# RWKV recurrence of a four-layer block: values and keys turned two chunks at a time, the score product kept whole, the inverse written through predicates

## The chip, the cores and the metric

The kernel runs on 1 core of one Trainium2 chip. The metric is the device time of one execution in microseconds. Before the change three runs gave 4173.98, 4181.47 and 4182.22 us; the median is 4181.47.

## The reference, cut to what matters

Two blocks run one behind the other, each with two layers, on 512 tokens of width 1024, all in float32. The change touches one stage of the second block only, which runs once in each of its two layers: the time mix of RWKV-7. For each of 16 heads of width 64 it computes

```python
def step(state, inp):                      # state is 64 x 64
    r_t, w_t, k_t, v_t, a_t, b_t = inp
    sa = einsum('bhvk,bhk->bhv', state, a_t)
    state = state * w_t[:, :, None, :] + sa[..., None] * b_t[:, :, None, :] \
            + v_t[..., None] * k_t[:, :, None, :]
    return state, einsum('bhvk,bhk->bhv', state, r_t)
```

The inputs r, w, k, v, a, b come from projections of the normed input, mixed with the token before. Behind the scan stand a group norm over each head, a bonus term and a gate.

## The kernel before, in words

**Tiling.** Features lie on the 128 partitions and the 512 tokens on the free axis, so a tile of 128x512 holds two heads. The stage works through 8 such pairs of heads (`PAIRS`), and the tokens in 8 chunks of 64 (`C`, `NC`). Within a chunk the recurrence is solved in closed form. With A the strictly triangular product of keys `a` and queries `at_` (the score product, `scores(p, 0)` and its transpose `scores(p, 1)`), the inverse of I - A is needed for all 8 chunks of both heads. It is built by doubling: `xx` holds the inverse of the diagonal blocks, `xt` its transpose, and each of five levels (`INV_LEVELS` 2, 4, 8, 16, 32) adds the off-diagonal blocks of one size.

**One level.** `lower(p, i)` multiplies the part `ct` of A that belongs to the level by `xx` (16 small matmuls, by `products`, L1954). ScalarE copies the result from bank 3 to `pp`. `inverse(p, i)` and `inverse_t(p, i)` multiply it by `xt` from the other side. VectorE adds bank 5 to `xx` (`add_x`, L2371) and bank 4 to `xt` (`add_xt`, L2375). `ct` itself is made by VectorE before each level, as `mabt` times a mask of zeros and ones (`next_ct`, L2366). The first `xx` and `xt` are a masked product plus the identity (two instructions each: L2360 and L2382, L2393 and L2396). The two strict score products, the three others and all masks have one instruction each, `keep_masked`, L2360.

**The chain.** Chunks of a pair depend on each other through `state`. Each chunk has three steps, so a pair has 24: `chain(p, i)` on TensorE (L1931 to L1947), and behind each a small VectorE instruction (`rhs` L2263, `uu` L2265, `state` L2268) that the next step waits for. The chain of pair p-1 is woven into the work of pair p: one step stands behind each of the products in TensorE's order, and the `step(...)` calls of VectorE stand at fixed places in its order. Both orders are written by hand and strictly in order. In what follows, steps 0, 3, 6, ... have the larger TensorE part (four groups, A), steps 1, 4, 7, ... the smallest (B), and steps 2, 5, 8, ... the third (C).

**One pair in TensorE's order.** First the dense part: small products for decay `w` and rate `a`, the projections of k and r (24 matmuls each, L228 to L230), a sum of squares (`ssq`), the projection of v, the gate g and a bonus sum. Then the scores: chain 0, `scores` 0, chain 1, `scores` 1, chain 2, `turned` 0, chain 3, `scores` 2 to 4 with chain 4 to 6 behind them. Then five levels, with `turned` 1 and 2 in the first two. `turned` brings v, b and k from features on partitions to tokens on partitions: 8 matmuls of a 128x64 piece each against a 128x128 matrix (L2015, L2017), into two banks, from which ScalarE copies four quarters (`keep_turned`).

**VectorE's order** for a pair is decays, keys (token shift of k), `kt`, `post(p - 2)` (group norm scale, bias and gate of an earlier pair, L2285 to L2288), the norm of the keys (L2341), shift of r, `at_` (L2350), `rt` (L2353), shift of v, step 0, then masks and levels. **ScalarE** carries the activations, the copies out of PSUM, and the negation of each weight piece (L161) that GpSimd's queue needs before it can add the raw weights on top (L132). **SyncE** loads masks at the stage's start (L1895) and two small tiles per pair.

Of the kernel before, what the change touches and what calls it, by code (L numbers as in the profile page):

```python
# [21 lines left out]
P = 128  # L22
# [1785 lines left out]
def rwkv_b(run, io, l, ws, again, nxt, y_all, y_hi, y_lo, gate):  # L1808

    with ExitStack() as ctx:  # L1810
# [9 lines left out]
        xx, ct = z[:, 0, 1:S + 1], z[:, 1, 1:S + 1]  # L1820
# [4 lines left out]
        lm, cen = sc.sb("lm", [P, 10, C]), sc.sb("cen", [P, P])  # L1825
# [17 lines left out]
        x_made, xt_made, c_ready = sc.sem("x_made"), sc.sem("xt_made"), sc.sem("c_ready")  # L1843
# [12 lines left out]
        for p in range(PAIRS):  # L1856
# [7 lines left out]
            for j in range(3):  # L1864
                order += [(f"t{j}", (p, h), h, p_free) for h in range(2)]
# [27 lines left out]
        def _(sp):  # L1893
            sc.enter_and_clear(sp)
            sp.dma_start(lm[:, :, :], io["b_lm"]).then_inc(const_in, 16)  # L1895
            sp.dma_start(bones[:, :], io["b_bones"]).then_inc(const_in, 16)
# [9 lines left out]
        def _(pe):  # L1906
# [12 lines left out]
            def chain(p, i):  # L1919
# [4 lines left out]
                if i % 3 == 0:  # L1924
                    if i == 0 and p:
                        pe.wait_ge(y_kept, p)
                    if i == 0:
                        pe.wait_ge(xt_made, 6 * (p + 1))
                        pe.wait_ge(*read("t2", (p, 1)))
# [27 lines left out]
            def dense(p):  # L1957
                def decays():
# [3 lines left out]
                    if p:  # L1962
                        pe.wait_ge(f_free, 5 * p)
                        pe.wait_ge(x_made, 5 * p)
# [26 lines left out]
            def scores(p, j):  # L1991
                b, f = p % 2, 5 * p + j
                lhs, rhs_ = ((a, at_[b]), (at_[b], a), (kt, at_[b]), (a, rt[b]), (kt, rt[b]))[j]
                if j == 0:
                    pe.wait_ge(at_made, p + 1)
                    pe.wait_ge(*read("w", p))
                elif j == 1:
                    pe.wait_ge(*read("ssq", p))
                else:
                    pe.wait_ge(f_free, f - 1)  # L2000
                if j == 3:
                    pe.wait_ge(rt_made, p + 1)
                products(2 + j % 2, lhs, rhs_, f_made)

            def turned(p, j):
# [81 lines left out]
            pe.wait_ge(f_free, 5 * PAIRS)  # L2087
# [19 lines left out]
        def _(act):  # L2107
# [36 lines left out]
            def decays(p):  # L2144
                act.wait_ge(lr_made, 2 * p + 1)
                if p:
                    act.wait_ge(c_ready, 5 * p)
# [18 lines left out]
            for p in range(PAIRS):  # L2166
# [34 lines left out]
                do(gg[:, p % 2, :], bank("g", p)[:, :], ACT.Copy, signal=read("g", p))  # L2201
                ws.high(st, n + 4)

                def keep_turned(j):
                    dst = (vt, bt, ktt)[j][p % 2]
                    act.wait_ge(tr_made, 3 * p + j + 1)
                    for i in range(4):

                        g, h = i // 2, i % 2
                        src = bank(f"t{j}", (p, g))[0:C, :].rearrange("p (c h k) -> p c h k", c=4, h=2)[:, :, h, :]  # L2210
                        out = dst[h * C:(h + 1) * C, g * 256:(g + 1) * 256].rearrange("p (c k) -> p c k", c=4)
                        do(out, src, ACT.Copy, signal=read(f"t{j}", (p, g)) if h else None)
# [16 lines left out]
            act.wait_ge(c_ready, LEVELS_ * PAIRS)  # L2229
# [21 lines left out]
        def _(dve):  # L2251
# [54 lines left out]
            dve.wait_ge(const_in, 48)  # L2306
            do(dve.scalar_tensor_tensor(out=cen[:, :], in0=bones[:, :], scalar=-1.0 / C, in1=run.eye[:, :],
                                        op0=ALU.mult, op1=ALU.add), (cen_made, 1))
            for p in range(PAIRS):
# [19 lines left out]
                if p:  # L2329
                    decays()  # L2330
                    keys()
# [6 lines left out]
                if p >= 2:  # L2338
                    post(p - 2)
# [13 lines left out]
                do(dve.tensor_tensor(rt[b], r, e0, ALU.mult), (rt_made, p + 1))  # L2353
                shift(f + 2, "v", p, v, col("mu_v", p))

                def keep_masked(j):

                    dst, m = ((mabt, 0), (xx, 2), (mak[b], 0), (mrb[b], 1), (mrk[b], 1))[j]
                    dve.wait_ge(f_made, 5 * p + j + 1)
                    do(dve.tensor_tensor(chunks(dst), chunks(banks[2 + j % 2][:, :]), each_chunk(lm[:, m, :]), ALU.mult),  # L2360
                       (f_free, 5 * p + j + 1))
# [39 lines left out]
                next_ct(1)  # L2401
# [5 lines left out]
                next_ct(2)  # L2407
# [5 lines left out]
                next_ct(3)  # L2413
# [4 lines left out]
                next_ct(4)  # L2418
# [600 lines left out]
def constants_b():  # L3019
# [17 lines left out]
    lm = [s < t, s <= t, level[1].T, level[1]] + [level[n] for n in INV_LEVELS] + [s == t]  # L3037
    lm = np.stack([m.astype(f) for m in lm], 1)
    bones = (row[:, None] // 64 == row[None, :] // 64).astype(f)
# [56 lines left out]
```

## Time and profile before

| | us |
|---|---|
| profiled execution | 4173.47 |
| its span | 4171.7 |
| three runs | 4173.98, 4181.47, 4182.22 |
| TensorE matmul busy | 3868.6 (93%) |
| VectorE busy | 2112.0 (51%) |
| ScalarE busy | 1712.1 (41%) |

The page gives each engine's busy time as a share of the span. TensorE's share counts overlapping matmuls with modelled ends, so 93% is not 93% of its peak. The time mix stage lies between about 1761 and 2290 us (layer 0) and 3072 and 3600 us (layer 1). In the 40 slices of the page VectorE stands at 6 tenths there, where TensorE stands at 8 and 9. In what follows pair 4 of layer 0 stands for the others: its dense part begins at 2001.13, its scores at 2024.74, and the next pair begins at 2059.98.

### The profile page before, as it was taken

Reading aid. Unit: us, or ns where it says so; the run is one execution under the profiler, and the core shown is the slowest. Engines: PE = TensorE matmul, PEld = TensorE weight load, DVE = VectorE, ACT = ScalarE, POOL = GpSimd, SP = SyncE. Lnnn points to the kernel's source line nnn. Section 1 sums busy time; section 2 is a strip of 40 time slices with the busy share of each in tenths; the row PEclk is TensorE's granted clock in tenths of the full one; section 3 lists DMA queues with packets and bytes.
Section 4 is the critical chain, followed back from the end, with each engine's and each line's share of the span. In section 5 each row is a group of like instructions: output and inputs, shape, how many; then the busy total and the mean of one; then the engine's idle time right before and its main releaser. Section 6 shows DMA issues by size and latency. Waiting matters only on the chain.

```text
span 4171.7 us, 70239 instructions
## 1 busy us (share of the span) xinstructions
PE 3868.6 (93%) x29148; PEld 3135.1 (75%) x29148; DVE 2112.0 (51%) x3719; ACT 1712.1 (41%) x2512; POOL 794.6 (19%) x1108
## 2 busy tenths in 40 slices
PE   5898999999899999999999999998999999989997
PEld 4676778777678877877787778876777787778885
DVE  5575662126533227366664376325546666356603
ACT  3264422336443236445443332235644444342223
POOL 1111222221122221210001222221120000222221
PEclk9999999999999999999999999999999999999998
DMA  8855998975489985832223879986572222679995
GB/s 282 236 118 106 272 292 188 199 171 120 95 175 193 191 172 119 177 86 66 53 52 87 182 161 195 193 183 146 115 170 66 52 55 57 142 153 196 193 191 130
DMA packets 189741, 628.75 MB, mean 151 GB/s; under 512 B 22768, under 2 KB 27888, under 8 KB 189040
## 3 DMA queue, kind: packets, MB, share of 16 engines
q0 software_dynamic: 158976, 549.52, 61.0%
q1 hardware_dynamic: 27888, 70.53, 4.9%
q8 instruction: 232, 3.80, 0.4%
q10 hardware_dynamic: 2560, 4.20, 0.3%
q14 instruction: 85, 0.70, 0.1%
HBM read 612.63 MB, written 2.10 MB: 147 GB/s over the span
## 4 chain that ended last, share of the span: by engine, by line
PE 42%; DVE 10%; ACT 6%; DMA 2%; issue 2%; SPq 0%; DVEq 0%; ACTq 0%; POOL 0%
PE bank L228 11%; PE bank L230 10%; PE bank L229 10%; PE bank L1954 4%; ACT L2112 1%; ACT gate L2112 1%; PE bank L1642 1%; PE bank L1624 1%; DVE rw_z L2371 1%; PE bank L1943 1%; ACT w L2112 1%; PE bank L2015 1%; ACT acc L2112 1%; PE bank L1615 1%; DVE x L392 1%
## 5 line engine op out<-in xcount | busy, mean ns | idle before, releaser
L228 PE MATMUL bank<-h_hi,w_hi 128*128 128x512 f32 x2608 | 1065.7, 409 | 46.4 <-DMA w_lo<-in_b_wup 7.9
L230 PE MATMUL bank<-h_hi,w_lo 128*128 128x512 f32 x2608 | 1024.6, 393 | 0.0
L229 PE MATMUL bank<-h_lo,w_hi 128*128 128x512 f32 x2608 | 1024.4, 393 | 0.0
L161 ACT ACTIVATE w_lo<-w_hi 128x1024 fp32r<-128x1024 f32 (+2 forms) x552 | 556.0, 1011 | 1002.5 <-DMA w_hi<-in_a_wgv 301.8
L228 PEld LDWEIGHTS bank<-h_hi,w_hi 128*128 128x128 f32 x2608 | 494.5, 190 | 180.5 <-issue 57.2
L229 PEld LDWEIGHTS bank<-h_lo,w_hi 128*128 128x128 f32 x2608 | 495.1, 190 | 106.5 <-issue 10.5
L230 PEld LDWEIGHTS bank<-h_hi,w_lo 128*128 128x128 f32 x2608 | 494.4, 190 | 106.9
L2112 ACT ACTIVATE gate<-bank 128x512 f32<-128x512 f32 x80 | 47.8, 597 | 277.1 <-PE bank L1954 277.1
L228 PE MATMUL bank<-fa_y_hi,w_hi 128*128 128x512 f32 x352 | 137.1, 390 | 1.8 <-DMA w_lo<-in_a_wd 1.8
L228 PE MATMUL bank<-fb_y_hi,w_hi 128*128 128x512 f32 x352 | 137.0, 389 | 0.7 <-DMA w_lo<-in_b_wd 0.7
L229 PE MATMUL bank<-fb_y_lo,w_hi 128*128 128x512 f32 x352 | 136.9, 389 | 0.0
L230 PE MATMUL bank<-fb_y_hi,w_lo 128*128 128x512 f32 x352 | 136.9, 389 | 0.0
L230 PE MATMUL bank<-fa_y_hi,w_lo 128*128 128x512 f32 x352 | 136.9, 389 | 0.0
L229 PE MATMUL bank<-fa_y_lo,w_hi 128*128 128x512 f32 x352 | 136.9, 389 | 0.0
L1388 DVE TENSOR_SCALAR fa_conv<-fa_a_in,par_a 128x512 f32<-128x512 f32 x44 | 21.6, 492 | 225.9 <-ACT fa_a_in L1334 225.5
L2637 DVE SCALAR_TENSOR_TENSOR fb_work<-fb_work,par_b 128x512 f32<-128x512 f32 x176 | 132.3, 752 | 6.3
L128 POOL DMA_DIRECT2D w_hi<-in_b_wrkv x48 | 31.5, 655 | 520.6 <-PE bank L230 520.6
L2634 DVE TENSOR_TENSOR fb_work<-bank,rstd 128x512 f32<-128x512 f32 x88 | 60.9, 692 | 124.5 <-PE bank L230 123.7
L2647 DVE COPY fb_work<-bank 128x512 f32<-128x512 f32 x16 | 11.1, 692 | 211.3 <-ACT w L319 211.3
L1421 DVE SCALAR_TENSOR_TENSOR x<-bank,mods,x 128x512 f32<-128x512 f32 x16 | 12.0, 751 | 207.1 <-PE bank L230 207.1
L132 POOL DMA_DIRECT2D w_lo<-in_a_wgv x96 | 90.3, 947 | 125.4 <-ACT w_lo L161 117.9
L132 POOL DMA_DIRECT2D w_lo<-in_b_wup x96 | 87.1, 914 | 115.3 <-ACT w_lo L161 108.1
(461 smaller groups left out, 7661.7 us busy)
## 6 DMA issues: line engine op xcount, KB each, us to landing
w_hi<-in_a_wgv POOLq DMA_DIRECT2D x80, 512.0 KB, 5.3
w_lo<-in_a_wgv POOLq DMA_DIRECT2D x80, 512.0 KB, 7.6
w_hi<-in_b_wup POOLq DMA_DIRECT2D x80, 512.0 KB, 5.2
w_lo<-in_b_wup POOLq DMA_DIRECT2D x80, 512.0 KB, 7.4
w_hi<-in_a_wh POOLq DMA_DIRECT2D x48, 512.0 KB, 4.7
w_lo<-in_a_wh POOLq DMA_DIRECT2D x48, 512.0 KB, 5.7
fa_ada_raw<-in_ada SPq DMA_DIRECT2D x48, 512.0 KB, 7.9
w_hi<-in_b_wrkv POOLq DMA_DIRECT2D x48, 512.0 KB, 4.9
```

What stands on the lines that cost most here:

```text
L132: pool.dma_start(self.lo[:, self.span(n)], self.pieces[n][0], accum_op=ALU.add)\
L161: st.do(st.eng.activation(self.lo[:, s], self.hi[:, s].bitcast(F32), ACT.Copy, scale=-1.0), (self.neg_made, n + 1))
L228: pe.matmul(out, self.hi[:, a], hh[:, k0 + k, :], start=first and k == 0, stop=False)
L229: pe.matmul(out, self.hi[:, a], hl[:, k0 + k, :], start=False, stop=False)
L230: mm = pe.matmul(out, self.lo[:, a], hh[:, k0 + k, :], start=False, stop=last and k == ks - 1)
L392: st.do(st.eng.scalar_tensor_tensor(out=run.x[:, k, :], in0=y, scalar=gain[:, k:k + 1], in1=run.x[:, k, :], op0=ALU.mult, op1=ALU.add), se ...
L1615: mm = pe.matmul(banks[2 + g][:, 256 * j:256 * (j + 1)], rot[rows, p % 2, ib * P:(ib + 1) * P], kpad[rows, kb, ib * P:(ib + 2) * P], start ...
L1624: mm = pe.transpose(banks[4 + i // 4][:, (i % 4) * P:(i % 4 + 1) * P], s[:, u % 3, i * P:(i + 1) * P], run.eye[:, :])
L1954: mm = pe.matmul(banks[out][s_, cut(c)], lhs[s_, cut(c)], rhs_[s_, cut(c)], start=True, stop=True)
L2112: st.do(act.activation(*args, **how), signal)
L2634: do(dve.tensor_tensor(a_in[:, b, 2:S + 2], banks[n % 4][:, :], run.rstd[:, :], ALU.mult), (a_free, n + 1))
L2637: do(dve.scalar_tensor_tensor(out=conv[:, b, :], in0=a_in[:, b, j:j + S], scalar=col(f"conv{j}", n), in1=conv[:, b, :], op0=ALU.mult, op1= ...
```

## The change

Four things, all in the time mix stage. (1) `turned` takes two chunks at once: 4 matmuls with 128 weight columns where there were 8 with 64, into one bank; the four copies of ScalarE keep their size. (2) ScalarE copies the first score product whole from bank 2 to `mabt`, with no mask, and `lower` multiplies all of it. (3) `xx` and `xt` are first filled with identities by ScalarE, and every later write to them is one `copy_predicated` under an integer mask, which takes only the blocks of that level; `ct`, its five masks and the two additions of the identity are gone. (4) In VectorE's order `post(p - 2)` moves from behind `kt` to ahead of the keys, and step 0 of the chain moves ahead of the shift of v. A new constant `im` (128 x 11 x 64, int32) is loaded at the stage's start, and `lm` shrinks from 10 masks to 3.

```diff
@@ rwkv_b: tiles and order
-        xx, ct = z[:, 0, 1:S + 1], z[:, 1, 1:S + 1]
+        xx = [z[:, i, 1:S + 1] for i in range(2)]
-        lm, cen = sc.sb("lm", [P, 10, C]), sc.sb("cen", [P, P])
+        lm, im, cen = sc.sb("lm", [P, 3, C]), sc.sb("im", [P, 11, C], I32), sc.sb("cen", [P, P])
...
-                order += [(f"t{j}", (p, h), h, p_free) for h in range(2)]
+                order.append((f"t{j}", p, j % 2, p_free))
...
@@ sync
             sp.dma_start(lm[:, :, :], io["b_lm"]).then_inc(const_in, 16)
+            sp.dma_start(im[:, :, :], io["b_im"]).then_inc(const_in, 16)
@@ tensor: scores(p, j), turned(p, j), lower(p, i)
                 elif j == 1:
                     pe.wait_ge(*read("ssq", p))
+                elif j == 2:
+                    pe.wait_ge(ab_made, p + 1)
+                elif j == 3:
+                    pe.wait_ge(x_made, LEVELS_ * p + 1)
+                    pe.wait_ge(rt_made, p + 1)
                 else:
-                    pe.wait_ge(f_free, f - 1)
-                if j == 3:
-                    pe.wait_ge(rt_made, p + 1)
+                    pe.wait_ge(f_free, 3 * p + 1)
...
-                outs = [claim(f"t{j}", (p, h)) for h in range(2)]
-                for c in range(NC):
-                    out = outs[c // 4][0:C, (c % 4) * P:(c % 4 + 1) * P]
+                whole_bank = claim(f"t{j}", p)
+                for i in range(NC // 2):
+                    out, two = whole_bank[:, i * P:(i + 1) * P], slice(i * P, (i + 1) * P)
                     if j == 0:
-                        mm = pe.matmul(out, v[:, cut(c)], cen[:, :], start=True, stop=True)
+                        mm = pe.matmul(out, v[:, two], cen[:, :], start=True, stop=True)
                     else:
-                        mm = pe.transpose(out, (e0, e1)[j - 1][:, cut(c)], run.eye[:, :])
+                        mm = pe.transpose(out, (e0, e1)[j - 1][:, two], run.eye[:, :])
...
                 pe.wait_ge(x_made, n + 1)
-                pe.wait_ge(c_ready, n + 1)
...
-                    pe.wait_ge(f_free, 5 * p + 4)
-                products(3, ct, xx, cx_made)
+                    pe.wait_ge(f_free, 3 * p + 2)
+                products(3, mabt, xx[p % 2], cx_made)
@@ scalar: for each pair, behind the copy of g
                 do(gg[:, p % 2, :], bank("g", p)[:, :], ACT.Copy, signal=read("g", p))
+                if p >= 2:
+                    act.wait_ge(ch_made, 24 * (p - 1))
+                else:
+                    act.wait_ge(const_in, 64)
+                do(chunks(xt[p % 2]), each_chunk(lm[:, 2, :]), ACT.Copy, signal=(one_made, 2 * p + 1))
+                act.wait_ge(z_free, f + 2)
+                do(chunks(xx[p % 2]), each_chunk(lm[:, 2, :]), ACT.Copy, signal=(one_made, 2 * p + 2))
+                act.wait_ge(f_made, 5 * p + 1)
+                do(mabt, banks[2][:, :], ACT.Copy, signal=(ab_made, p + 1))
                 ws.high(st, n + 4)
...
@@ vector: for each pair
                 if p:
                     decays()
+                    if p >= 2:
+                        post(p - 2)
                     keys()
...
                 do(dve.tensor_tensor(kt, kp, e1, ALU.mult))
-                if p >= 2:
-                    post(p - 2)
...
                 do(dve.tensor_tensor(rt[b], r, e0, ALU.mult), (rt_made, p + 1))
+                step(0)
                 shift(f + 2, "v", p, v, col("mu_v", p))
...
-                    dst, m = ((mabt, 0), (xx, 2), (mak[b], 0), (mrb[b], 1), (mrk[b], 1))[j]
+                    dst, m = ((mak[b], 0), (mrb[b], 1), (mrk[b], 1))[j - 2]
...
-                def next_ct(i):
-                    if i:
-                        dve.wait_ge(cx_made, LEVELS_ * p + i)
-                    do(dve.tensor_tensor(chunks(ct), chunks(mabt), each_chunk(lm[:, 4 + i, :]), ALU.mult),
-                       (c_ready, LEVELS_ * p + i + 1))
+                def put(dst, m, src, signal):
+                    do(dve.copy_predicated(chunks(dst), each_chunk(im[:, m, :]), chunks(src)), signal)
+
+                def first_x():
+                    dve.wait_ge(f_made, 5 * p + 2)
+                    dve.wait_ge(one_made, 2 * p + 2)
+                    put(xx[b], 0, banks[3][:, :], (x_made, LEVELS_ * p + 1))
+
+                def first_xt():
+                    dve.wait_ge(ab_made, p + 1)
+                    put(xt[b], 5, mabt, (xt_made, 6 * p + 1))
                 def add_x(i):
                     dve.wait_ge(xcx_made, 4 * p + i + 1)
-                    do(dve.tensor_tensor(xx, xx, banks[5][:, :], ALU.add), (x_made, LEVELS_ * p + i + 2))
+                    put(xx[b], 1 + i, banks[5][:, :], (x_made, LEVELS_ * p + i + 2))
                 def add_xt(i):
                     dve.wait_ge(xcxt_made, LEVELS_ * p + i + 1)
-                    do(dve.tensor_tensor(xt[b], xt[b], banks[4][:, :], ALU.add), (xt_made, 6 * p + i + 2))
+                    put(xt[b], 6 + i, banks[4][:, :], (xt_made, 6 * p + i + 2))
-                one = each_chunk(lm[:, 9, :])
-                step(0)
-                keep_masked(0)
                 step(1)
-                keep_masked(1)
-                do(dve.tensor_tensor(chunks(xx), chunks(xx), one, ALU.add), (x_made, LEVELS_ * p + 1))
+                first_x()
                 step(2)
-                next_ct(0)
+                first_xt()
...
-                do(dve.tensor_tensor(chunks(xt[b]), chunks(mabt), each_chunk(lm[:, 3, :]), ALU.mult))
...
-                do(dve.tensor_tensor(chunks(xt[b]), chunks(xt[b]), one, ALU.add), (xt_made, 6 * p + 1))
...
-                next_ct(1)
...
-                next_ct(2)
...
-                next_ct(3)
...
-                next_ct(4)
@@ constants_b
-    lm = [s < t, s <= t, level[1].T, level[1]] + [level[n] for n in INV_LEVELS] + [s == t]
+    lm = [s < t, s <= t, s == t]
+    im = [level[n].T for n in (1,) + INV_LEVELS[:-1]] + [level[n] for n in (1,) + INV_LEVELS]
```

## Rows read from the trace of the kernel before

**Rows 1.** Busy time by stretch: pair 4's dense part, its scores and levels, pair 1, layer 1
```profile
2001.13:2024.74 23.61, 22.25 (x90) 15.55 (x86) 13.68 (x20) 18.72 (x25) 2.83 (x5) 1.00 0.27 68
2024.74:2059.98 35.24, 32.59 (x889) 30.13 (x888) 24.71 (x52) 8.71 (x19) 1.45 (x3) 1.00 0.25 54
...
1849.70:1884.80 35.10, 32.46 (x891) 30.10 (x890) 23.10 (x50) 8.29 (x18) 0.88 (x1) 1.00 0.23 51
...
3072.00:3600.00 528.00, 497.12 (x8016) 407.21 (x8015) 317.55 (x586) 237.50 (x369) 46.98 (x66) 1.00 0.32 73
```

**Rows 2.** The chain of waits through pair 4 of layer 0: start, length, what
```profile
2009.41 0.64 ACT acc L2112
...
2016.27 0.76 DVE y_all L2285
2018.57 0.70 DVE w L2341
...
2025.76 0.70 DVE gate L2277
...
2053.59 0.61 ACT gate L2112
```

**Rows 3.** Groups by form of VectorE: count, busy and mean, idle before
```profile
L2366 DVE TENSOR_TENSOR rw_z<-gate,rw_lm 128x512 f32<-128x512 f32 x80 | 55.4, 693 | 5.6 <-PE bank L1954 2.7 <-DVE rw_rhs L2263 0.2 <-DVE rw_state L2268 0.2
...
L1163 DVE COPY_PREDICATED ma_kept<-ma_masks,bank 128x512 f32<-128x512 int32 x56 | 41.6, 743 | 9.1 <-PE bank L951 3.2 <-DVE ma_decay L1181 0.5
```

**Rows 4.** Timeline of pair 4, VectorE and ScalarE ahead of the scores
```profile
2013.30 0.69 DVE L2277 TENSOR_TENSOR gate<-rw_z 128x512 f32<-128x512 f32 x1 [6.26 <-ACT rw_z L2112]
...
2017.22 0.61 ACT L2112 ACTIVATE rw_z<-bank 128x512 f32<-128x512 f32 x1
...
2024.40 0.60 ACT L2112 ACTIVATE rw_gg<-bank 128x512 f32<-128x512 f32 x1
```

**Rows 5.** Timeline of pair 4, weight loads of TensorE, scores to level 2
```profile
2024.74 0.20 PEld L1931 LDWEIGHTS bank<-rw_state,rw_at 64*64 64x64 f32 x4 [0.76 <-issue]
2025.20 1.06 PEld L1954 LDWEIGHTS bank<-rw_at,gate 64*64 64x64 f32 x32
...
2027.55 0.19 PEld L1939 LDWEIGHTS bank<-rw_rhs,rw_xt 64*64 64x64 f32 x4 [1.28 <-DVE rw_rhs L2263]
2028.59 0.20 PEld L1943 LDWEIGHTS bank<-rw_mrb,rw_uu 64*64 64x64 f32 x4
...
2029.14 1.72 PEld L2015 LDWEIGHTS bank<-rw_cen,gate 128*64 128x64 f32 x16
...
2031.03 0.20 PEld L1931 LDWEIGHTS bank<-rw_state,rw_at 64*64 64x64 f32 x4 [0.17 <-issue]
...
2043.74 0.80 PEld L2017 LDWEIGHTS bank<-eye,w 128*64 128x64 f32 x8
...
2047.85 1.06 PEld L1954 LDWEIGHTS bank<-rw_z 64*64 64x64 f32 x32
```

**Rows 6.** Timeline of pair 4, one level of the inverse (level 3)
```profile
2052.35 1.06 PEld L1954 LDWEIGHTS bank<-rw_z 64*64 64x64 f32 x32
...
2053.28 0.25 PEld L1931 LDWEIGHTS bank<-rw_state,rw_at 64*64 64x64 f32 x4
...
2054.24 1.01 PEld L1954 LDWEIGHTS bank<-gate,rw_xt 64*64 64x64 f32 x32 [0.36 <-ACT gate L2112]
...
2055.17 0.20 PEld L1939 LDWEIGHTS bank<-rw_rhs,rw_xt 64*64 64x64 f32 x4
...
2055.28 1.02 PEld L1954 LDWEIGHTS bank<-rw_xt,gate 64*64 64x64 f32 x32
...
2055.51 0.69 DVE L2371 TENSOR_TENSOR rw_z<-rw_z,bank 128x512 f32<-128x512 f32 x1 [0.66 <-PE bank L1954]
...
2056.51 0.20 PEld L1943 LDWEIGHTS bank<-rw_mrb,rw_uu 64*64 64x64 f32 x4 [0.21 <-DVE rw_uu L2265]
```

**Rows 7.** Timeline, a run of full-width f32 matmuls in an earlier stage
```profile
352.37 1.05 PE L951 MATMUL bank<-ma_sw 128*128 128x128 f32 x8
```

More of the change, by code:

```diff
@@ L1842, in rwkv_b @@
         f_made, f_free, tr_made = sc.sem("f_made"), sc.sem("f_free"), sc.sem("tr_made")
-        x_made, xt_made, c_ready = sc.sem("x_made"), sc.sem("xt_made"), sc.sem("c_ready")
+        x_made, xt_made = sc.sem("x_made"), sc.sem("xt_made")
+        ab_made, one_made = sc.sem("ab_made"), sc.sem("one_made")
         cx_made, cx_kept, xcx_made, xcxt_made = (sc.sem("cx_made"), sc.sem("cx_kept"), sc.sem("xcx_made"),
@@ L1928, in chain @@
                         pe.wait_ge(xt_made, 6 * (p + 1))
-                        pe.wait_ge(*read("t2", (p, 1)))
+                        pe.wait_ge(*read("t2", p))
                     for s_ in heads:
@@ L1962, in decays @@
                     if p:
-                        pe.wait_ge(f_free, 5 * p)
+                        pe.wait_ge(f_free, 3 * p)
                         pe.wait_ge(x_made, 5 * p)
@@ L1991, in scores @@
             def scores(p, j):
-                b, f = p % 2, 5 * p + j
+                b = p % 2
                 lhs, rhs_ = ((a, at_[b]), (at_[b], a), (kt, at_[b]), (a, rt[b]), (kt, rt[b]))[j]
@@ L2086, in last_var @@
                     whole("var", PAIRS - 1, bones[:, :], yq[:, :], var_made)
-            pe.wait_ge(f_free, 5 * PAIRS)
+            pe.wait_ge(f_free, 3 * PAIRS)
             pe.wait_ge(x_made, 5 * PAIRS)
@@ L2146, in decays @@
                 if p:
-                    act.wait_ge(c_ready, 5 * p)
+                    act.wait_ge(cx_made, 5 * p)
                 st.settle()
@@ L2207, in keep_turned @@
                     for i in range(4):
[L2209 to L2212, printed above, removed]
+                        q, h = i // 2, i % 2
+                        src = bank(f"t{j}", p)[q * C:(q + 1) * C, :].rearrange("p (c h k) -> p c h k", c=4, h=2)
+                        out = dst[h * C:(h + 1) * C, :].rearrange("p (c two k) -> p c two k", c=4, two=2)
+                        do(out[:, :, q, :], src[:, :, h, :], ACT.Copy, signal=read(f"t{j}", p) if i == 3 else None)
                 keep_turned(0)
@@ L2228, in _ @@
             keep_y(PAIRS - 2)
-            act.wait_ge(c_ready, LEVELS_ * PAIRS)
+            act.wait_ge(cx_made, LEVELS_ * PAIRS)
             act.wait_ge(xcxt_made, LEVELS_ * PAIRS)
@@ L2305, in _ @@
             shift(2, "low", 2, gd[:, 1, :], col("mu_g", 1))
-            dve.wait_ge(const_in, 48)
+            dve.wait_ge(const_in, 64)
             do(dve.scalar_tensor_tensor(out=cen[:, :], in0=bones[:, :], scalar=-1.0 / C, in1=run.eye[:, :],
@@ L2353, in _ @@
                 do(dve.tensor_tensor(rt[b], r, e0, ALU.mult), (rt_made, p + 1))
+                step(0)
                 shift(f + 2, "v", p, v, col("mu_v", p))
                 def keep_masked(j):
-                    dst, m = ((mabt, 0), (xx, 2), (mak[b], 0), (mrb[b], 1), (mrk[b], 1))[j]
+                    dst, m = ((mak[b], 0), (mrb[b], 1), (mrk[b], 1))[j - 2]
                     dve.wait_ge(f_made, 5 * p + j + 1)
                     do(dve.tensor_tensor(chunks(dst), chunks(banks[2 + j % 2][:, :]), each_chunk(lm[:, m, :]), ALU.mult),
-                       (f_free, 5 * p + j + 1))
@@ L2363, in next_ct @@
-                def next_ct(i):
-                    if i:
-                        dve.wait_ge(cx_made, LEVELS_ * p + i)
-                    do(dve.tensor_tensor(chunks(ct), chunks(mabt), each_chunk(lm[:, 4 + i, :]), ALU.mult),
-                       (c_ready, LEVELS_ * p + i + 1))
+                       (f_free, 3 * p + j - 1))
+                def put(dst, m, src, signal):
[4 more added lines that the diff above has]
+                    put(xx[b], 0, banks[3][:, :], (x_made, LEVELS_ * p + 1))
@@ L3036, in constants_b @@
         level[n] = same & (s % (2 * n) < n) & (t % (2 * n) >= n)
-    lm = [s < t, s <= t, level[1].T, level[1]] + [level[n] for n in INV_LEVELS] + [s == t]
+    lm = [s < t, s <= t, s == t]
     lm = np.stack([m.astype(f) for m in lm], 1)
+    im = [level[n].T for n in (1,) + INV_LEVELS[:-1]] + [level[n] for n in (1,) + INV_LEVELS]
+    im = np.stack([m.astype(np.int32) for m in im], 1)
     bones = (row[:, None] // 64 == row[None, :] // 64).astype(f)
@@ L3041, in constants_b @@
     reset[:, ::C] = 0.0
-    return {"b_freq": freq, "b_band": band, "b_lm": np.concatenate([lm, lm]), "b_bones": bones, "b_reset": reset}
+    return {"b_freq": freq, "b_band": band, "b_lm": np.concatenate([lm, lm]), "b_im": np.concatenate([im, im]), "b_bones": bones, "b_reset": reset}
 def arrays_b(inp):
```

## The prediction

> **What bounds the kernel now.** I read the windows first, then the chain of waits inside one pair, then the timeline. Only the time mix stage is touched, about 528 us in each of two layers [rows 1]. Pair 4 splits into a dense part of 23.61 us and 35.24 us of scores, levels and chain steps; pair 1 takes 35.10 for the latter [rows 1]. In neither part is one engine simply full. In the second, matmuls are recorded busy for 32.59 of 35.24 us, but a small matmul's record outlasts its slot in the queue: a group of 16 (a "product") starts at 2052.35 and the next instruction at 2053.28, so it costs 0.93 of TensorE's order, although its weight loads alone are recorded at 1.06 [rows 6]. The chain of waits passes back and forth: ScalarE's variance work and VectorE's `post` and norm, a shift of v, then in the levels ScalarE's copy [rows 2]. So the reader is to see a loop between three in-order queues, where an edit is worth what the last wait at each place loses.
>
> **Prices.** From starts of weight loads: product 0.93; step A 0.46 (2024.74 to 2025.20) [rows 5]; step B 0.11 (2055.17 to 2055.28) [rows 6]; step C I take at 0.34 from the same pace. From a product's start to a reader: 1.27 on VectorE (2054.24 to 2055.51), 1.24 on ScalarE (2052.35 to 2053.59) [rows 2, 6]. A masked product on VectorE costs 0.693, a predicated copy of 128x512 from PSUM under an int32 mask 0.743: the same form runs 56 times in an earlier stage [rows 3]. ScalarE's copy of a bank costs 0.61 [rows 2].
>
> **Part 1, turned in pairs.** `turned` 0 holds the order from 2029.14 to 2031.03, 1.89 for 16 records; a transposing one records 0.80 for its 8 loads, some 0.95 of the order [rows 5]. Half the matmuls of the same moving width is half of that, if twice the weight columns cost nothing. A run of 8 full-width f32 records took 1.05 including the last one's latency [rows 7], which is a pace no worse than 0.12. So 0.95, 0.5 and 0.5: it saves 1.9 a pair. Bounds: nothing saved (weights twice as long in the way) and 1.9. I take the latter, since the full-width row is the same instruction. The Trainium skill ("TensorE: Matmul & The Clock Gate", section "LDWEIGHTS (loading the stationary operand)") says that a weight load takes time in proportion to its columns, whatever the contraction. By that rule eight loads of 64 columns and four of 128 cost the same, and wherever loads set the pace this part would save nothing; the full-width row, at the pace of the half-width one, speaks for loads that are hidden.
>
> **Part 2, the front of the pair.** Today `post` (2.3 us, 2016.27 to 2018.57) stands between `kt` and the norm [rows 2]. Its input is ready at 2010.05 (ScalarE's exponential from 2009.41) [rows 2], and VectorE idles 6.26 us until 2013.30 [rows 4]. Moved there, `post` ends near 2012.4 and is hidden with 0.9 to spare; were that cover gone, it would cost what it overruns. What is late next is the copy of r, from 2017.22 to 2017.83 [rows 4]: the shift of r can start at 2017.9 where it started 2.3 - 0.9 = 1.4 later. The whole train behind it moves up by about 1.5, so `at_` ends near 2023.5 and `rt` near 2024.2, before TensorE leaves the dense part, which stays at 2024.74. Today `at_`, `rt` and the shift of v run until 2027.25, and only then comes step 0 (the wait of 1.28 ahead of 2027.55) [rows 2, 5]. After: step 0 at 2025.33 to 2025.55, shift of v to 2027.05, step 1 to 2027.30. TensorE: A 2024.74, `scores` 0 2025.20, B 2026.13, `scores` 1 2026.25, then C waits for step 1 until 2027.36. It began at 2028.59 [rows 5]: 1.23 gained. `turned` 0 then ends at 2028.65 where it ended at 2031.03 [rows 5], 1.15 more (0.95 of it part 1, the rest a gap of 0.2 ahead of it).
>
> **Part 3, scores 2 to level 2.** VectorE loses ten instructions (two masked first products, the masked first `xt`, two identity additions, five `ct`), gains two predicated writes, and nine additions become predicated: so 19 instructions of 0.693 become 11 of 0.743, 13.2 becomes 8.2 us [rows 3]. ScalarE gains three copies, 1.9 us. Walked in order with the prices above: step 3 at 2028.65, `scores` 2 at 2029.11, B 2030.05, `scores` 3 2030.16, then C waits 0.45 for step 4 (which stands behind the third mask, ready at 2031.24) until 2031.55; `scores` 4 2031.89, A 2032.83, level 0 2033.29, B 2034.23, `turned` 1 2034.34, C 2035.13 (0.29 waited), inverse 2035.47, A 2036.41, its transpose 2036.87, B 2037.81, level 1 2037.92, C 2039.19 (0.33), `turned` 2 2039.53, A 2040.25, and so on to level 2 at 2043.37. From the end of `turned` 0 that is 14.7 us; before, from 2031.03 to 2047.85, 16.82 [rows 5]. Gained: 2.1, of it 0.95 part 1.
>
> **Part 4, levels 2 to 4.** Nothing is gained. A level takes 4.50 (2047.85 to 2052.35) [rows 5, 6]; its waits are ScalarE's copy (0.36 ahead of 2054.24) and `uu` behind `add_x` (0.21 ahead of 2056.51) [rows 6]. `ct` lay in VectorE's idle time. Both waits stay, and `add_x` as a predicated copy is 0.05 longer: 0.15 lost a pair, three levels.
>
> **Moves that I cost at nothing.** ScalarE's three copies stand behind the copy of g (2024.40) [rows 4]. The two identities are read first at 2027.5 and 2028.6 and made by 2026.0; `mabt` is made at 2027.05 and `scores` 2 comes at 2029.11. Slack 1.5 to 2 us; if it were gone, each microsecond would hold `scores` 2 and all behind it by one, some 15 us in all. Behind ScalarE's new waits (previous chain, shift of r, `scores` 0) stand one negation L161 and GpSimd's L132, both 2 us later, for weights used 30 us on. `scores` 2 now waits for `mabt`, with chain 4 behind it; `scores` 3 for `xx`, ready at 2028.3. The mask load adds one DMA of 360 KB to SyncE's queue ahead of the others, while the weight queue has a third of the DMA time [rows 1]; the first use of a predicate comes over 40 us later in layer 0.
>
> **Sum.** Walk per pair 24.74 to 55.65 against 24.74 to 59.98: 1.23 + 1.15 + 2.1 - 0.15 = 4.3 us. But the same walk made over the kernel before gives 34.3, 0.9 short of 35.24 [rows 1]; the rest are short gaps, ahead of `turned` above all, which the change will not remove. I charge 0.6 of it: 3.75 a pair. Six pairs (2 to 7) give 22.5; pair 1, without `post`, 3.5 (35.10 against 30.9 + 0.6) [rows 1]; pair 0 has no chain, so only part 1 less the longer adds, 1.5. That is 27.5 a layer, 55 in both. The profiled execution took 4173.5, 8 us under the median of 4181.5 and level with the fastest of the three runs: 4118.5 by the one, 4126.5 by the other. I give the middle, 4122.
>
> **Rivals.**
> *Half of it (4148).* The full-width weight load isn't hidden: part 1 saves nothing, 1.9 a pair over 16 pairs, 30 us less. The row for full width [rows 7] speaks against; for it, that row's operands are other tiles and its run is short. The same size would follow if ScalarE's slack at `scores` 2 were overrun by 2 us.
> *More of it (4105).* The gaps go too, because fewer claims and waits stand ahead of `turned`: 4.3 to 4.7 a pair, 15 us more.
> *Nothing (4178).* The loop is set by the chain of `state` alone, so that each step waits for the one before. Against: in rows 6 TensorE waits 0.36 and 0.21 in 4.5, the rest is its own work.
> *Slower (4212).* The predicated copy is dearer here than the 0.743 of its twin, since the mask repeats every 64 elements and the target is read and written in place. Its price stands in the wait of every `uu` and `rhs`. Walking with 1.0 gives 32.5 a pair, with 1.2 34.0, and at 1.25 the gain of VectorE is spent (34.3 for the old kernel by the same walk). At twice 0.743, 1.5, the walk is 36.5, 2.2 longer a pair, 30 us in all. Against it speaks only that row, but it differs in nothing else.
>
> **Chances.** Forecast 0.62, half 0.17, more 0.12, nothing 0.04, slower 0.05. About 0.2% (8 us) is what a measurement can tell from no change. Faster by more 0.91, within 0.04, slower 0.05. The range takes in "more" with 5 us for which level of the runs is met, and "half": 4096 to 4150.
>
> **What would show it.** `turned` 0 in half its time; C(2) within 2.7 us of A(0) where it was 3.85; predicated copies at 0.74 to 0.75; levels 2 to 4 at 4.5 to 4.6 as before; the second part of a pair at 31.5; dense part unchanged at 23.6; stage near 500 us. I am wrong if the dense part grows (`post` in the way of the keys), if ScalarE ends the wait of `scores` 2, or if the stages behind give back what the recurrence gained, since their weights must still be loaded.

## The result, and the profile after

The changed kernel takes 4121.16 us (median of 4 runs, 4118.63 to 4127.93), the kernel before 4177.73 beside it (4 runs, 4172.39 to 4182.22): the recorded ratio is 0.9876, with a 95% interval of 0.9862 to 0.9889 (the quotient of the two medians is 0.9865). The profiled execution took 4121.49 us where that of before took 4173.5, 52 us less.

The stretches of the changed kernel, in the columns of [rows 1]: pair 4's dense part, pair 4's scores and levels, those of pair 5. The granted clock of TensorE is 1.00 in each, as in [rows 1], so it has no part in the difference.

```profile
1986.59:2010.27 23.68, 22.27 (x91) 15.56 (x87) 14.67 (x21) 19.05 (x26) 3.39 (x5) 1.00 0.30 71
2010.27:2042.61 32.34, 30.36 (x873) 28.34 (x872) 18.67 (x42) 10.26 (x21) 0.87 (x1) 1.00 0.24 56
2065.95:2097.27 31.32, 30.21 (x873) 28.26 (x873) 18.69 (x42) 10.26 (x21) 0.87 (x1) 1.00 0.25 57
```

The dense part is where it was (23.61 to 23.68) and all the gain lies behind it: 35.24 to 32.34 in pair 4, and 31.32 in pair 5; pair 4 holds one gap of 1.02 us that pair 5 lacks. Over the twelve pairs 1 to 6 of both layers the median of the second part is 31.46, and 34.93 before. Pair 0 falls from 46.8 and 47.38 (its two layers) to 44.72 and 44.75. From the start of pair 0 to the start of pair 7 the stage is 22.9 and 22.2 us shorter (394.77 and 394.2 to 371.86 and 372.01); on to the last step A, pair 7 and its chain bring 3.8 and 3.5 more. That makes 52.4 us, and the 52.0 of the span follow from it only because the rest nearly cancels: between the two stages the changed kernel takes 6.5 us longer (816.9 for 810.3), ahead of the first 1.8 us less and behind the second 4.3 us less (575.9 for 580.3). Over the thirteen kernels of this document, which are built alike there, these stretches lie between 810 and 818 and between 574 and 580 us, in one profiled execution each. So the gain of the stages is not visibly given back, but no run excludes that a few us of it are.

The weight loads of TensorE in pair 4 answer to [rows 5]: from step A of chunk 0 to the next step A, and then the start of level 2 and of level 3.

```profile
2010.27 0.20 PEld L1933 LDWEIGHTS bank<-rw_state,rw_at 64*64 64x64 f32 x4 [0.76 <-issue]
2010.73 1.06 PEld L1956 LDWEIGHTS bank<-rw_at,gate 64*64 64x64 f32 x32
2011.66 0.25 PEld L1941 LDWEIGHTS bank<-rw_rhs,rw_xt 64*64 64x64 f32 x4
2012.90 0.19 PEld L1945 LDWEIGHTS bank<-rw_mrb,rw_uu 64*64 64x64 f32 x4
2013.44 0.97 PEld L2020 LDWEIGHTS bank<-rw_cen,gate 128*128 128x128 f32 x8
2014.53 0.20 PEld L1933 LDWEIGHTS bank<-rw_state,rw_at 64*64 64x64 f32 x4
...
2021.40 0.42 PEld L2022 LDWEIGHTS bank<-eye,w 128*128 128x128 f32 x4
...
2030.38 1.06 PEld L1956 LDWEIGHTS bank<-rw_z,gate 64*64 64x64 f32 x32
...
2034.59 0.19 PEld L1945 LDWEIGHTS bank<-rw_mrb,rw_uu 64*64 64x64 f32 x4 [0.26 <-DVE rw_uu L2278]
...
2034.93 1.06 PEld L1956 LDWEIGHTS bank<-rw_z,gate 64*64 64x64 f32 x32
```

Step B has no wait any more, where 1.28 stood ahead of it, and so step C follows 2.63 after step A (3.85 before). `scores` 2 (the product behind the step A of 2014.53) has no wait for ScalarE's copy either. `turned` 0 holds the order for 1.09 (2013.44 to 2014.53; 1.89 before), a transposing one records 0.42 for 4 loads (0.80 for 8). Level 2 takes 4.55 (2030.38 to 2034.93; 4.50 before) and waits 0.26 for `uu` (0.21 before).

VectorE's timeline of the pair shows `post` (the tail of a group norm, its first instruction L2298) in what was idle time, step 0 at 2010.85, and the first predicated copy:

```profile
1995.30 0.75 DVE L2298 SCALAR_TENSOR_TENSOR y_all<-y_all,par_b,acc 128x512 f32<-128x512 f32 x1 [3.09 <-ACT acc L2116]
...
2010.85 0.23 DVE L2276 COPY rw_rhs<-bank 128x64 f32<-128x64 f32 x1 [1.00 <-PE bank L1934]
...
2013.07 0.74 DVE L2378 COPY_PREDICATED rw_z<-rw_im,bank 128x512 f32<-128x512 int32 x1 [0.23 <-PE bank L1956]
2013.85 0.28 DVE L2281 SCALAR_TENSOR_TENSOR rw_state<-rw_state,rw_ec,bank 128x64 f32<-128x64 f32 x1
```

The groups of predicated copies (count, busy, mean in ns, idle before them), from a bank and from `mabt` in SBUF, and ScalarE's copies of the ones:

```profile
L2378 DVE COPY_PREDICATED rw_z<-rw_im,bank 128x512 f32<-128x512 int32 x80 | 59.0, 737 | 82.8 <-PE bank L1956 82.8
L2378 DVE COPY_PREDICATED rw_xt<-rw_im,bank 128x512 f32<-128x512 int32 x80 | 58.9, 736 | 24.1 <-PE bank L1956 21.8
L2378 DVE COPY_PREDICATED rw_xt<-rw_im,gate 128x512 f32<-128x512 int32 x16 | 11.8, 736 | 0.6
L2116 ACT ACTIVATE rw_z<-rw_lm 128x512 f32<-128x512 f32 x16 | 10.1, 632 | 1.5
```

What TensorE waits for in the time mix stage of layer 0 (total us, times, longest), first in the kernel before:

```profile
PE bank L1939 <- DVE rw_rhs L2263: 7.9, 13, 1.2
...
PE bank L1943 <- DVE rw_uu L2265: 2.6, 7, 0.4
...
PE bank L1931 <- DVE rw_state L2268: 2.0, 8, 0.5
```

and after. The wait for `rhs`, 1.2 us once in each of pairs 2 to 7, is the one that went. The listed waits for VectorE fall by 11 us in eight pairs and the stage by 26.7: the rest is TensorE's own work and waits too short for this view.

```profile
PE bank L1956 <- ACT gate L2116: 5.2, 17, 0.7
...
PE bank L1941 <- DVE rw_rhs L2276: 1.1, 7, 0.2
PE bank L1933 <- DVE rw_state L2281: 0.5, 1, 0.5
```

### The profile page after: what moved, and what is told of

It is laid out like the page before. It is cut to its first block, busy times and chain, and to the rows that moved or that the text cites. A ratio compares the mean times of both kernels' runs of the same rounds, so it can differ in the third digit from the quotient of the medians.

```text
span 4119.7 us, 69619 instructions
## 1 busy us (share of the span) xinstructions
PE 3838.9 (93%) x28892; PEld 3113.2 (76%) x28892; DVE 2031.1 (49%) x3591; ACT 1740.7 (42%) x2560; POOL 792.4 (19%) x1108
## 4 chain that ended last, share of the span: by engine, by line
PE 48%; ACT 5%; DVE 5%; DMA 2%; issue 1%; SPq 0%; ACTq 0%; DVEq 0%; POOL 0%
PE bank L228 11%; PE bank L230 11%; PE bank L229 11%; PE bank L1956 5%; ACT gate L2116 1%; PE bank L1642 1%; PE bank L1919 1%; PE bank L1945 1%; ACT L2116 1%; PE bank L1624 1%; DVE rw_z L2378 1%; PE bank L1615 1%; DMA at_sw<-at_raw 1%; ACT acc L2116 1%; PE bank L1933 0%
## 5 line engine op out<-in xcount | busy, mean ns | idle before, releaser
L2116 ACT ACTIVATE gate<-bank 128x512 f32<-128x512 f32 x96 | 57.3, 597 | 267.0 <-PE bank L1956 266.8
L319 ACT ACTIVATE w<-x 128x512 f32<-128x512 f32 x72 | 45.5, 632 | 151.0 <-DVE x L1421 72.0
```

Source lines behind the costliest of these rows:

```text
L319: st.do(st.eng.activation(self.run.w[:, k % 2, :], src, ACT.Square), self.sig("sq", 8 * part + k + 1))
L2116: st.do(act.activation(*args, **how), signal)
```

## The experiments

For each kernel I read off the weight loads the time from one step A (line 1931 or 1933) to the next: eight segments a pair. Medians over the twelve pairs 1 to 6; the first segment holds `scores` 0 and 1 and `turned` 0, the second `scores` 2 to 4, the third the start of level 0 and `turned` 1, the fourth the rest of level 0, the start of level 1 and `turned` 2, then the later levels. "sum" adds the eight medians, so it leaves out gaps that stand in a few pairs only.

```
kernel        A0-A3 -A6  -A9  -A12 -A15 -A18 -A21 -end  sum   time us  ratio to before, 95%
before        6.29  4.09 4.99 4.31 4.05 4.50 4.50 2.20  34.93 4177.73
after         4.26  4.06 3.64 3.96 4.10 4.55 4.55 2.20  31.32 4121.16  0.9876 0.9862-0.9889
only_turned   5.96  4.18 4.97 3.90 4.05 4.50 4.50 2.20  34.26 4160.62  0.9982 0.9972-0.9991
only_order    5.79  4.05 5.01 4.31 4.05 4.50 4.50 2.20  34.41 4165.46  0.9987 0.9975-0.9998
only_masks    6.28  4.05 3.99 4.36 4.10 4.55 4.55 2.20  34.08 4160.21  0.9972 0.9962-0.9981
no_turned     5.07  4.05 3.99 4.36 4.10 4.55 4.54 2.20  32.86 4147.53  0.9945 0.9928-0.9961
no_order      5.46  4.06 3.65 3.96 4.10 4.55 4.55 2.20  32.53 4143.01  0.9925 0.9899-0.9951
no_masks      5.13  4.18 4.97 3.90 4.05 4.50 4.50 2.20  33.43 4154.31  0.9952 0.9935-0.9968
twice         4.68  5.01 3.64 5.11 5.44 5.44 5.44 2.17  36.93 4209.45  1.0080 1.0054-1.0107
uu_first      4.26  4.06 3.64 3.61 4.03 4.27 4.28 2.17  30.32 4109.43  0.9843 0.9818-0.9868
both_orders   4.26  3.93 3.58 3.61 4.02 4.12 4.15 2.20  29.87 4109.44  0.9863 0.9845-0.9881
no_post       4.67  4.18 3.65 3.96 4.10 4.55 4.55 2.20  31.86 4138.97  0.9928 0.9908-0.9948
no_step0      4.08  4.07 3.64 3.96 4.10 4.55 4.55 2.20  31.15 4121.64  0.9887 0.9867-0.9907
```

The kernel before ran again beside each set of experiments (medians 4173.12, 4171.68 and 4167.65; 4177.73 beside the changed kernel), and the ratio is to those runs. So a difference in us between two rows can be off by up to 10 us where the rows come from different sets; there the ratios and the segments decide.

**One part alone.** My theory was the loop between queues; the rivals were that TensorE's work or VectorE's work alone sets the time.

only_turned, the kernel before with pairs of chunks turned:

```diff
-                for c in range(NC):
-                    out = outs[c // 4][0:C, (c % 4) * P:(c % 4 + 1) * P]
+                for i in range(NC // 2):
+                    out, two = whole_bank[:, i * P:(i + 1) * P], slice(i * P, (i + 1) * P)
```

> The kernel before with part 1 alone (chunks turned in pairs). Loop theory (a step is worth what the last wait at its place loses): TensorE gets 1.9 us a pair back, but VectorE is the late one until level 2, so the second part of a pair falls only from 34.9 to 34.3, pair 0 keeps its 1.5 to 2, and the whole is 10 to 14 us faster than before. TensorE theory (93% busy, its work decides): the full 1.9 x 16 = 30 us.

Second part 34.29, so 0.64 a pair of the 1.9 of TensorE's order that the part takes out. The medians lie 12.5 us apart, inside what the loop theory gave; the ratio says 7.5 us (4 to 12). Both exclude the 30 us of the TensorE theory. The weight loads of pair 4 in it show where the rest goes:

```profile
2022.34 0.19 PEld L1939 LDWEIGHTS bank<-rw_rhs,rw_xt 64*64 64x64 f32 x4 [1.29 <-DVE rw_rhs L2263]
...
2023.93 0.97 PEld L2015 LDWEIGHTS bank<-rw_cen,gate 128*128 128x128 f32 x8
2025.51 0.20 PEld L1931 LDWEIGHTS bank<-rw_state,rw_at 64*64 64x64 f32 x4 [0.61 <-DVE rw_state L2268]
```

`turned` 0 is short, and the next step A then waits 0.61 for `state`: VectorE hands on late.

only_order, the kernel before with `post` ahead of `keys` and step 0 ahead of the shift of v:

```diff
+                    if p >= 2:
+                        post(p - 2)
                     keys()
...
+                step(0)
                 shift(f + 2, "v", p, v, col("mu_v", p))
```

> The kernel before with the two moves in VectorE's order alone (post ahead of the keys, chain step 0 ahead of the shift of v). Loop theory: the first wait goes (1.2 us), but the two masked products and the identity behind it take most of it back, second part 34.9 to 34.4, 5 to 8 us in all. Rival, the front's gain is kept whole: 1.2 x 14 = 17 us.

34.41, as the walk had it; the first segment falls by 0.5, and the medians lie 7.7 us apart (5 us by the ratio), where the rival had 17.

only_masks, the kernel before with `mabt` and the ones by ScalarE and predicated copies:

```diff
-                    do(dve.tensor_tensor(xx, xx, banks[5][:, :], ALU.add), (x_made, LEVELS_ * p + i + 2))
+                    put(xx[b], 1 + i, banks[5][:, :], (x_made, LEVELS_ * p + i + 2))
```

> The kernel before with the masks' part alone (whole score product kept by ScalarE, identities by ScalarE, predicated copies). Loop theory: VectorE has 5 us less a pair, but it starts late into the scores (step 0 stands behind post and the shift) and TensorE has the long turned; second part 34.9 to 34.1, 9 to 13 us in all. VectorE theory (its work in this stage decides): 5 us x 16 x most of it, 50 us or more, nearly all of what the change brought.

34.08. Five microseconds less of VectorE's work a pair are worth 0.85 and 13 us in all, where the rival that counts VectorE's work had 50 or more: it falls. The gain lies in one segment (4.99 to 3.99). The first doesn't move, since the 1.27 ahead of step B is still there.

**One part taken back from the changed kernel.** If the parts simply added, taking one out would cost what it brought alone.

no_turned (the `-` and `+` lines of only_turned exchanged):

> The changed kernel with the old turned (8 matmuls of 64 columns). Loop theory: VectorE is early now, so TensorE's 1.9 us count nearly whole: second part 31.4 to 33.2, 25 to 30 us slower than the changed kernel (4147 to 4152). If the three parts simply add up, it loses what part 1 alone brings, 10 to 14 us.

no_order (those of only_order exchanged):

> The changed kernel with VectorE's old order (post behind kt, step 0 behind the shift of v). Loop theory: second part 31.4 to 32.7, 14 to 18 us slower than the changed kernel (4135 to 4139). If the parts add up: it loses only what the moves alone bring, 5 to 8 us.

no_masks (the old masks, `ct` and additions, the rest of the change kept):

```diff
-                    put(xx[b], 1 + i, banks[5][:, :], (x_made, LEVELS_ * p + i + 2))
+                    do(dve.tensor_tensor(xx, xx, banks[5][:, :], ALU.add), (x_made, LEVELS_ * p + i + 2))
```

> The changed kernel with the old masks, ct and additions (parts 1 and the order kept). Loop theory: second part 31.4 to 33.6, 30 to 35 us slower than the changed kernel (4151 to 4156). VectorE theory: nearly all of the 56 us is gone. If the parts add up: 9 to 13 us slower.

Taken out, the parts cost 1.5, 1.2 and 2.1 a pair (no_turned, no_order, no_masks against after), near what the loop theory had for each (1.8, 1.3 and 2.2); alone they bring 0.67, 0.52 and 0.85. So they don't add: alone 2.0 together, the whole change 3.6. By the medians the three are 26, 22 and 33 us slower than the changed kernel; no_order was expected at 14 to 18, and 22 (20 by the ratio) lies above that. The rival in no_masks, that nearly all of the gain is VectorE's work and goes with it, falls: 33 of some 57 us went. The ratios say the same of the sum: 0.18, 0.13 and 0.28% alone, 0.69, 0.49 and 0.76% taken out, 1.24% in all. The first segment shows it best: 6.29 falls by 0.33, 0.50 and 0.01 with one part, and by 2.03 with all three. It ends with the later of two things, TensorE's own order (with its wait for `rhs`) and `state` from VectorE, and each part shortens only one. In no_masks the waits show the shift: ahead of step B 1.1 in all is left, but ahead of step C, which needs `uu` from a VectorE busy with masks, there is now 10.6 (2.6 before):

```profile
PE bank L1943 <- DVE rw_uu L2265: 10.6, 20, 0.8
...
PE bank L1939 <- DVE rw_rhs L2263: 1.1, 7, 0.2
```

**The two moves apart.** no_post puts `post` back behind `kt` and leaves step 0 where the change has it:

```diff
-                    if p >= 2:
-                        post(p - 2)
...
                 do(dve.tensor_tensor(kt, kp, e1, ALU.mult))
+                if p >= 2:
+                    post(p - 2)
```

> The changed kernel with post back behind kt, step 0 still ahead of the shift of v. The walk: at_ late again by 1.4, but step 0 at once behind rt, so step C(2) waits 0.4 more; second part 31.4 to 31.8, 6 us slower than the changed kernel. Rival (the prediction's text put the 1.23 down to both moves together): most of the 1.3 is lost, second part 32.7.

no_step0 puts only step 0 back behind the shift of v:

```diff
-                step(0)
                 shift(f + 2, "v", p, v, col("mu_v", p))
...
+                step(0)
                 step(1)
```

> The changed kernel with step 0 back behind the shift of v, post still moved. The walk: with at_ early, the shift of v ends near 2025.8 on pair 4's clock and step 0 still comes before TensorE has finished the first score product; no loss, second part 31.3 to 31.4, within 2 us of the changed kernel. Rival: step 0's place is what brought the gain, second part 32.7.

With step 0 behind the shift nothing is lost in time (4121.64 us), and the first segment is even 0.18 shorter (4.08 for 4.26): in the changed kernel VectorE stands idle for 1.00 until TensorE's step A is through (the row of 2010.85). Only then comes the shift of v, and `uu` behind it is a little late for step C, which follows 2.63 after step A in the changed kernel and 2.45 in no_step0. With `post` back 0.54 of segment time a pair and 18 us in all (22 by the ratio) are lost, at least three times what I expected in time. The two profiled executions place most of it: the span is 16.8 us longer, 13.6 of it in the two stages. Pairs 1 to 6 hold 9.2 (6.5 by the segments, the rest is gaps put down to "issue", of which no_post has eight over 0.25 us and the changed kernel three), pair 7 3.3 and pair 0 1.4. Both moves back cost 1.2 a pair, though: once `post` is late, step 0's place matters. Pair 1, which has no `post` ahead of it, is the cross-check: in no_order its first segment takes 4.08 where the other pairs take 5.46, in no_post 4.27 where they take 4.67. no_post's timeline of pair 4 shows `rt` (L2366) running until 2016.22 with step 0 on its heels; the step would have had to stand behind the whole shift of v:

```profile
2015.27 0.20 PEld L1933 LDWEIGHTS bank<-rw_state,rw_at 64*64 64x64 f32 x4 [0.76 <-issue]
...
2015.53 0.69 DVE L2366 TENSOR_TENSOR rw_rt<-gate,w 128x512 f32<-128x512 f32 x1
...
2016.26 0.22 DVE L2276 COPY rw_rhs<-bank 128x64 f32<-128x64 f32 x1
...
2018.30 0.19 PEld L1945 LDWEIGHTS bank<-rw_mrb,rw_uu 64*64 64x64 f32 x4 [0.46 <-DVE rw_uu L2278]
```

**The price of the predicated copy.** twice makes each of them two times:

```diff
-                    do(dve.copy_predicated(chunks(dst), each_chunk(im[:, m, :]), chunks(src)), signal)
+                    for sig in (None, signal):
+                        do(dve.copy_predicated(chunks(dst), each_chunk(im[:, m, :]), chunks(src)), sig)
```

> The changed kernel with each predicated copy made twice (the second writes the same again), 1.5 us in place of 0.74, the price at which I said that the change turns slower. Loop theory: second part 31.4 to 37.0, 80 to 90 us slower than the changed kernel, 25 to 35 slower than the kernel before. Rival: VectorE has idle time in the levels that takes up the second copy (5 us of idle a pair), under 30 us slower than the changed kernel.

88 us slower than the changed kernel (85 by the ratio), 0.8% slower than before; 36.93 a pair, and the wait of step C for `uu` now leads:

```profile
PE bank L1945 <- DVE rw_uu L2278: 27.4, 35, 1.2
PE bank L1933 <- DVE rw_state L2281: 9.4, 29, 0.5
```

This was the prediction's slower case with its price of 1.5 made true, and the walk held: 36.5 plus the 0.6 charged, and 4212 us. The point at which the gain is spent, put at a price of 1.25, was not run.

**A better order.** In a level `uu` stood on VectorE behind `add_x`. uu_first puts steps 10, 13, 16 and 19 ahead of the copy that they stood behind:

```diff
                 step(9)
+                step(10)
                 add_xt(0)
-                step(10, 11)
+                step(11)
                 step(12)
-                add_x(1)
                 step(13)
+                add_x(1)
                 add_xt(1)
                 step(14, 15)
-                add_x(2)
                 step(16)
+                add_x(2)
                 add_xt(2)
                 step(17, 18)
-                add_x(3)
                 step(19)
+                add_x(3)
                 add_xt(3)
```

> The changed kernel with the chain's copy (uu) ahead of the predicated write of xx or xt in levels 1 to 3 and once in level 0. Loop theory: the wait of 0.24 to 0.26 ahead of step C goes, and the next product still finds xx ready or misses it by under 0.1: 0.2 to 0.3 us in four places, second part 31.4 to 30.5, 10 to 14 us faster than the changed kernel. Rival: the product waits for xx by as much as the chain gained, no change.

30.32 a pair, 1.0 less than the changed kernel, and 4109.43 us. On VectorE in level 2 `uu` comes first, and step C follows 1.05 after step B (2032.24), where it took 1.39 in the changed kernel (2033.20 to 2034.59); from step A to step A it is 4.26 (4.55):

```profile
2030.56 0.20 PEld L1933 LDWEIGHTS bank<-rw_state,rw_at 64*64 64x64 f32 x4
...
2032.24 0.20 PEld L1941 LDWEIGHTS bank<-rw_rhs,rw_xt 64*64 64x64 f32 x4
...
2032.70 0.22 DVE L2278 COPY rw_uu<-bank 128x64 f32<-128x64 f32 x1 [1.33 <-PE bank L1941]
2032.95 0.73 DVE L2378 COPY_PREDICATED rw_z<-rw_im,bank 128x512 f32<-128x512 int32 x1
2033.29 0.20 PEld L1945 LDWEIGHTS bank<-rw_mrb,rw_uu 64*64 64x64 f32 x4
...
2034.82 0.20 PEld L1933 LDWEIGHTS bank<-rw_state,rw_at 64*64 64x64 f32 x4
```

both_orders also takes step 4 ahead of the third mask, and in levels 2 and 3 lets TensorE take two chain steps before the product that waits for ScalarE (VectorE's steps 17 and 20 move ahead of a copy to match):

```diff
+                    if i in (2, 3):
+                        chain_on()
+                        inverse(p, i)
+                        chain_on()
+                        inverse_t(p, i)
+                        continue
...
-                keep_masked(2)
                 step(4)
+                keep_masked(2)
```

> uu_first, and in addition chain step 4 ahead of the third mask on VectorE, and in levels 2 and 3 on TensorE a second chain step ahead of the product that waits for ScalarE's copy. Loop theory: the wait of 0.3 ahead of C(5) goes, and step B fits into the wait for the copy, so second part 30.4 to 29.4 (levels 2 and 3 from 4.3 to 4.1 each), 12 to 17 us faster than uu_first, 4093 to 4100. Rival: the levels are bound by product, copy, product, write of xx, so that only step 4's 0.3 shows (5 us).

29.87, half of the 1.0 that I expected over uu_first: levels 2 and 3 give 0.15 and 0.13, step 4 gives 0.13, since the score behind it then waits for the mask. The 12 to 17 us expected in time did not come: 4109.44 against 4109.43. Gaps took back what the segments gained; with them the median of the second part is 30.36 here and 30.39 in uu_first. So uu_first is the version to keep. Its ratio lies below the changed kernel's, but the intervals overlap a little (up to 0.9868 against 0.9862 upwards), and the two come from different sets; the 12 us rest on the 1.0 a pair of the segments and on the two stages, which are 12.5 us shorter in its profiled execution.

## Why the prediction was right

The forecast was 4122, the time is 4121.16. That they agree within 1 us is luck: executions of the changed kernel alone spread over 9 us, and the forecast was the middle of two levels 8 us apart. What was right is the size, 52 to 57 us, and the walk behind it. By its steps:

- *Prices.* The predicated copy 0.737 for 0.743, ScalarE's copy of the ones 0.632 for 0.61. Right.
- *Part 1.* `turned` 0 holds the order 1.09 where I had 0.95, and the 0.2 between step C and it stayed (2012.90 to 2013.44 is 0.54, as 2028.59 to 2029.14 in [rows 5]). Here the first segment is 4.26 and the walk had 3.91. The doubled weights cost next to nothing: in `turned` 0 the records of 64 columns start 0.109 apart, those of 128 columns 0.111. So the first reason of "half of it" is excluded; the second, ScalarE late for `scores` 2, is too, since no wait of TensorE for ScalarE stands ahead of it in any pair. By the section "LDWEIGHTS (loading the stationary operand)" of the page "TensorE: Matmul & The Clock Gate" in the Trainium skill, eight loads of 64 columns would take as long as four of 128. The records here don't halve the spacing with the columns (0.42 for four of 128 against 0.80 for eight of 64), and one record lasts 0.192 for 128 columns and 0.137 for 64. So twice the columns did not slow TensorE's queue here; what sets the spacing, and whether the load inside a record follows the rule, no run here shows.
- *Part 2.* Right in size: step C 2.63 after step A, 2.62 forecast. Wrong in part of its cause: the text credits the moves of `post` and of step 0 together, and beside the first the second brings nothing and costs 0.18 of the first segment (no_step0); it would matter only without the first (no_order against no_post, 0.67 a pair). The train behind `post` moved up by so much that `rt` and the shift of v are out of the way by themselves.
- *Part 3.* From the end of `turned` 0 to level 2: 2014.53 to 2030.38 is 15.85, 14.83 without the gap of 1.02; the walk had 14.7. The gain is smaller than the 2.1 forecast all the same, 1.7: the 16.82 of the kernel before holds a gap of its own in pair 4 (0.30, put down to "issue", ahead of 2034.29), which the median pair lacks.
- *Part 4.* A level went from 4.50 to 4.55, the 0.05 forecast.
- *Sum.* 3.61 less a pair by segments, 3.47 by the median of the second part, 3.38 by its mean over pairs 1 to 6, 3.75 forecast (3.5 in pair 1). The walk of 30.9 measures 31.32 without gaps and the same walk of 34.3 measures 34.93, so it is short on both sides. Of the 4.3 that it gives, the first segment brought 2.0 for 2.4 and Part 3 1.7 for 2.1: together about the 0.6 that the sum charged for gaps. That charge was not spent on gaps: those put down to "issue" and over 0.25 us come to 2.0 us in the twelve pairs before and 2.1 after, some 0.2 a pair in both. Pair 0 seems sized too low at 1.5, with 2.1 and 2.6 measured, but it scatters: the six kernels that do the same work there (after, no_order, uu_first, both_orders, no_post, no_step0) have it between 44.4 and 46.7 (mean 45.35 of twelve), before and only_order between 46.7 and 47.4 (mean 46.98 of four), which is 1.6. In all the two stages brought 52.4 us where the sum had 55.
- *Rivals.* "Half", "nothing" and "more" are off by 27, 57 and 16 us. "Slower" named a mechanism that works, as twice shows, but the price of the copy stayed at that of its twin in [rows 3].

What the sum didn't say, though the walk contains it, is that the three parts need each other; whoever had added them up one by one from the parts' own runs would have come to 2.0 a pair.

## What to carry to other kernels

Where in-order queues hand work round a loop, walk the whole order once with prices from the trace; a part's gain alone says little of its gain beside the others (0.67 or 1.5 us a pair for the same edit here). On the queue that others wait for, let the short copy that releases them go ahead of the long one that nobody needs yet: four such exchanges brought 1.0 us a pair, some 12 us, with no instruction saved. A mask and an addition can be one predicated copy at the price of one instruction, if the fixed part is written beforehand by an engine with time to spare.

## What was not expected of the hardware

- Eight records of f32 weight loads of 128 columns take 0.97 together and hold the order 1.09 (2013.44 to 2014.53); sixteen of 64 columns took 1.72 and 1.89 [rows 5]. They start 0.111 and 0.109 apart.
- A predicated copy of 128x512 takes 736 to 737 ns from a PSUM bank and from SBUF alike.
- Gaps put down to "issue" stand in the second parts of every kernel, one to eight of over 0.25 us in the twelve pairs 1 to 6, the longest of 1.57. Their places are not random: counted in weight loads from the start of the program, the gap of 1.02 in pair 4 stands ahead of load 11379 (the first is 0), and a gap of 0.83 to 1.57 stands ahead of the same load in no_order, uu_first, both_orders, no_post and no_step0. Two of them in one pair are 127 loads apart (no_post three times, uu_first once). The profile has a DMA queue 8 of the kind `instruction`, with 230 packets of 16 KB in the changed kernel for TensorE's 57,784 loads and matmuls (some 251 each). All 46 gaps of the thirteen traces end 1.2 to 1.6 us after such a packet has landed, the one of pair 4 at 2020.67 after a landing at 2019.31; only 7 to 8% of all loads in the second parts start at such a distance from one. That points to TensorE waiting for its own instructions. No run was aimed at it, and why a packet is late is open.

```profile
2019.05 0.60 PEld L1956 LDWEIGHTS bank<-rw_z,gate 64*64 64x64 f32 x17
2020.67 0.48 PEld L1956 LDWEIGHTS bank<-rw_z,gate 64*64 64x64 f32 x14 [1.02 <-issue]
q8 instruction: 230, 3.77, 0.4%
```
